# Normalized probabilities computed by GpSimd, block choice one token tile later, three slots of scores: one stage of a two-layer trunk

## The chip, the cores and the metric

The kernel runs on one core of a Trainium2 chip. The time is device microseconds of one execution of the whole program. All times of the profile are microseconds from the start of the span unless marked ns. The engines are TensorE (PE, and PEld for its weight loads), VectorE (DVE), ScalarE (ACT), GpSimd (POOL) and SyncE (SP), which issues the transfers.

## The reference, cut to what matters

The program computes two transformer layers over 1024 tokens of width 1024. The change sits in the second layer's mixer, in the part that attends to compressed keys and chooses blocks of keys for the attention that follows:

```
n_cmp = (S - CMP_LEN) // CMP_STRIDE + 1                      # 63 compressed keys
s_c = einsum('bgjtd,bgnd->bgjtn', q, k_cmp) * scale - slopes * dist_c
s_c = where(dist_c >= 0, s_c, -inf)
e_c = exp(s_c - max(s_c)); l_c = sum(e_c)
p_c = e_c / where(l_c > 0, l_c, 1.0)
o_cmp = einsum('bgjtn,bgnd->bgjtd', p_c, v_cmp)
importance = einsum('bgjtn,nm->bgtm', p_c, overlap)          # 16 blocks of 64 keys
score = where(blk > cur, -inf, where(forced, inf, importance))
top_s, top_i = top_k(score, 8)
```

There are 16 heads in 4 groups (g) of 4 (j), and all arithmetic here is fp32.

## The kernel before, in words

The program is a row of stages, one behind the other. Each ends when all its engines and its last transfer have ended, and the next stage's first transfers are issued only then. The change touches one stage, compress_select_stage. Its first part (projection of the compressed keys and values) is left as it is. Its second part is a loop over 8 token tiles of 128 tokens (i = 0 to 7), with 128 tokens in the partitions and 16 heads x 64 compressed keys = 1024 columns. The engines run it side by side, each through its own instruction list in a fixed order, tied by semaphores. The work of tile i, with the short names that this text uses and the lines of the profile:

- bias(i), GpSimd, L2036 to L2045: the distance penalty and the mask, into one of two slots.
- S(i), TensorE, `scores`, L2094: 8 products of queries and compressed keys into ps_s (two slots of PSUM).
- M(i), VectorE, `maxima`, L2222 and L2225: adds the bias into s (SBUF, two slots), and takes the maximum of each head.
- E(i), ScalarE, `exps`, L2166: 16 exponentials in place in s, one per head, each with its row sum.
- R(i), VectorE, first part of `normalize`, L2230 and L2236 (L2234 for tile 0): reciprocal of the sums, and a copy of it.
- N(i), VectorE, last instruction of `normalize`, L2240: s times the reciprocal, into pn (two slots).
- T(i), TensorE, `transposes`, L2104: 8 transposes of pn into ps_t (one slot).
- K(i), ScalarE, `take`, L2174: ps_t copied to pt in SBUF.
- V(i), TensorE, `values`, L2114: 8 products of pt and the compressed values into ps_o (one slot).
- C(i), VectorE, `pick`, L2250 to L2268, only for i = 4 to 7: group sums of pn, scores of the blocks, the best eight, and a mask in sel.
- O(i), VectorE, `output`, L2275: ps_o times the gates, into the stage's result.

The lists of the loop are, one iteration i:

```
VectorE   R(i) N(i)  C(i) if i >= 4  O(i-1)  M(i+2)      (M(0) M(1) in front; O(7) behind)
TensorE   T(i)  V(i-1)  S(i+2)                           (S(0) S(1) in front; V(7) behind)
ScalarE   E(i)  K(i-1)
GpSimd    bias(i+2)                                      (bias(0) bias(1) in front)
```

At the end TensorE transposes sel (L2130) when all choices are made, ScalarE copies that to blocks (L2183), and SyncE writes blocks to memory (L2011). That transfer is the stage's last work.

Of the kernel before, what the change touches and what calls it, by code (L numbers as in the profile page):

```python
# [20 lines left out]
ALU = mybir.AluOpType  # L21
ACT = mybir.ActivationFunctionType
AX = mybir.AxisListType

P = 128
# [1900 lines left out]
def compress_select_stage(nc, kvT, pe, w1, w2, k_gain, gate_cols, qT, gates, selT, mixed, ident, slopes):  # L1926
# [12 lines left out]
    with Stage(nc, "cmpsel") as st:  # L1939
# [18 lines left out]
        bias = st.sb("bias", [P, 2, C_HEADS, CMP_PAD])  # L1958
        alive = st.sb("alive", [P, 1])
        force = st.sb("force", [P, TT, N_SLC])  # L1960
        s, pn = (st.sb(x, [P, 2, C_HEADS, CMP_PAD]) for x in ("s", "pn"))
        pt = st.sb("pt", [P, 2, PAIRS, P])
        top1, rowsum, rl, rla = (st.sb(x, [P, 2, C_HEADS]) for x in ("top1", "rowsum", "rl", "rla"))
        both = st.sb("both", [P, G, 1 + CMP_PAD])
# [49 lines left out]
        @block.gpsimd  # L2014
        def _(pool):
            nc.gpsimd.memset(t_in[HD:P, :, 0:COLS].rearrange("p v (g t) -> p v g t", t=SEQ)[:, :, :, SEQ - HALF:SEQ], 0.0).then_inc(tail_set, 1)
            pool.wait_ge(tail_set, 1)
            nc.gpsimd.memset(t_in[:, :, COLS + HALF:COLS + 2 * HALF], 0.0).then_inc(tail_set, 1)
            pool.wait_ge(tail_set, 2)
            nc.gpsimd.memset(kcp[:], 0.0).then_inc(zeroed, 1)  # L2020
            nc.gpsimd.memset(vcp[:], 0.0).then_inc(zeroed, 1)
            for h in range(C_HEADS):
                ins = nc.gpsimd.memset(nslope[:, h:h + 1], -slopes[h])
            ins.then_inc(slopes_set, 1)
            nc.gpsimd.memset(alive[:], 1.0).then_inc(alive_set, 1)
            pool.wait_ge(alive_set, 1)
            nc.gpsimd.affine_select(out=alive[:], in_=alive[:], compare_op=ALU.is_ge, fill=0.0, base=-(CMP_LEN - 1),
                                    pattern=[[0, 1]], channel_multiplier=1).then_inc(alive_set, 1)
            nc.gpsimd.memset(both[:], 0.0).then_inc(both_set, 1)
            nc.gpsimd.memset(blocks[:].bitcast(F32), 0.0).then_inc(blocks_set, 1)  # L2030
            pool.wait_ge(slopes_set, 1)

            def make_bias(i):
                if i >= 2:
                    pool.wait_ge(biased, i - 1)
                nc.gpsimd.iota(dist_i[:, i % 2, :], pattern=[[-CMP_STRIDE, CMP_PAD]], base=i * P - (CMP_LEN - 1),  # L2036
                               channel_multiplier=1).then_inc(dist_done, 1)
                pool.wait_ge(dist_done, 2 * i + 1)
                nc.gpsimd.tensor_copy(dist[:, i % 2, :], dist_i[:, i % 2, :]).then_inc(dist_done, 1)
                pool.wait_ge(dist_done, 2 * i + 2)  # L2040
                nc.gpsimd.tensor_tensor(bias[:, i % 2, :, :],
                                        dist[:, i % 2, :].rearrange("p (o n) -> p o n", o=1).to_broadcast([P, C_HEADS, CMP_PAD]),
                                        bcast(nslope[:].rearrange("p (h o) -> p h o", o=1), CMP_PAD), ALU.mult).then_inc(bias_step, 1)
                pool.wait_ge(bias_step, i + 1)
                nc.gpsimd.affine_select(out=bias[:, i % 2, :, :], in_=bias[:, i % 2, :, :], compare_op=ALU.is_ge, fill=NEG,  # L2045
                                        base=i * P - (CMP_LEN - 1), pattern=[[0, C_HEADS], [-CMP_STRIDE, CMP_PAD]],
                                        channel_multiplier=1).then_inc(bias_done, 1)

            make_bias(0)
            make_bias(1)  # L2050
            for i in range(TT):
                if i + 2 < TT:
                    make_bias(i + 2)

        @block.tensor
        def _(te):
# [61 lines left out]
            scores(0)  # L2118
            scores(1)
            for i in range(TT):  # L2120
                transposes(i)
                if i:
                    values(i - 1)
                if i + 2 < TT:
                    scores(i + 2)
            values(TT - 1)
            te.wait_ge(biased, TT)
            te.wait_ge(sel_done, TT - FIRST)
# [5 lines left out]
        @block.scalar  # L2134
        def _(act):
            act.wait_ge(peT_ready, 1)
            nc.scalar.activation(t_in[:, :, COLS:COLS + HALF], ps_t[:, 1, 0:2 * HALF].rearrange("p (v l) -> p v l", v=2), ACT.Copy)\
                .then_inc(peT_done, 1)
            for v in range(2):
                act.wait_ge(hid_ready, v + 1)  # L2140
                nc.scalar.activation(pb[:, v:v + 1], ps_s[:, 0, v * BANK + NW:v * BANK + NW + 1], ACT.Copy).then_inc(pb_done, 1)
                act.wait_ge(pb_done, v + 1)
                of = ps_s[:, 0, v * BANK:v * BANK + NW]
                if v == 0:
                    nc.scalar.activation(hid_k[:], of.rearrange("p (g n) -> p g n", g=G), ACT.Silu, bias=pb[:, 0:1]).then_inc(hid_done, 1)
                else:
                    nc.scalar.activation(hid_v[:, :, 0, :], of.rearrange("p (g n) -> p g n", g=G), ACT.Silu, bias=pb[:, 1:2])
                    nc.scalar.activation(hid_v[:, :, 1, :], of.rearrange("p (g n) -> p g n", g=G), ACT.Silu, bias=pb[:, 1:2])\
                        .then_inc(hid_done, 1)
            act.wait_ge(c_ready, 1)  # L2150
            nc.scalar.activation(sq[:], ps_o[0:CMP_PAD, 0, 0:G * HD].rearrange("p (g d) -> p g d", d=HD), ACT.Square).then_inc(sq_done, 1)
            act.wait_ge(norm, 2)
            nc.scalar.activation(root[:], ms[:], ACT.Sqrt).then_inc(norm, 1)
            act.wait_ge(g_in, 16)
            nc.scalar.activation(gates[:], g_raw[:], ACT.Sigmoid).then_inc(norm, 1)
            act.wait_ge(c_ready, 2)
            act.wait_ge(zeroed, 2)
            for half in range(2):
                rows = slice(half * HD, half * HD + HD)
                nc.scalar.activation(vcp[rows, :, rows], ps_o[rows, 1, 0:G * HD].rearrange("p (g d) -> p g d", d=HD), ACT.Copy)\  # L2160
                    .then_inc(vcp_done, 1)

            def exps(i):
                act.wait_ge(top1_done, i + 1)
                for h in range(C_HEADS):
                    ins = nc.scalar.activation(s[:, i % 2, h, :], s[:, i % 2, h, :], ACT.Exp, bias=top1[:, i % 2, h:h + 1],  # L2166
                                               accum_out=rowsum[:, i % 2, h:h + 1])
                ins.then_inc(e_done, 1)

            def take(i):  # L2170
                act.wait_ge(t_done, i + 1)
                if i >= 2:
                    act.wait_ge(o_done, i - 1)
                nc.scalar.activation(pt[:, i % 2, :, :], ps_t[:].rearrange("p b (m c) -> p (b m) c", c=P), ACT.Copy).then_inc(pt_done, 1)  # L2174

            for i in range(TT + 1):
                if i < TT:
                    exps(i)
                if i:
                    take(i - 1)  # L2180
            act.wait_ge(selT_ready, 1)
            act.wait_ge(blocks_set, 1)
            nc.scalar.activation(blocks[:, FIRST * P:SEQ], ps_s[0:G * N_SLC, 0, 0:SEQ - FIRST * P], ACT.Copy).then_inc(selT_taken, 1)  # L2183

        @block.vector
        def _(dve):
# [30 lines left out]
            def maxima(i):  # L2217
                dve.wait_ge(s_done, i + 1)
                dve.wait_ge(bias_done, i + 1)
                if i >= 2:  # L2220
                    dve.wait_ge(pn_done, i - 1)
                nc.vector.tensor_tensor(s[:, i % 2, :, :], ps_s[:, i % 2, :].rearrange("p (h n) -> p h n", n=CMP_PAD),  # L2222
                                        bias[:, i % 2, :, :], ALU.add).then_inc(biased, 1)
                dve.wait_ge(biased, i + 1)
                nc.vector.tensor_reduce(top1[:, i % 2, :], s[:, i % 2, :, :], AX.X, ALU.max, negate=True).then_inc(top1_done, 1)  # L2225

            def normalize(i):
                at = 2 * i
# [5 lines left out]
                    nc.vector.tensor_scalar(rla[:, 0, :], rl[:, 0, :], alive[:, 0:1], None, ALU.mult).then_inc(link, 1)  # L2234
                else:
                    nc.vector.tensor_copy(rla[:, i % 2, :], rl[:, i % 2, :]).then_inc(link, 1)  # L2236
                dve.wait_ge(link, at + 2)
                if i >= 2:
                    dve.wait_ge(t_done, i - 1)
                nc.vector.tensor_tensor(pn[:, i % 2, :, :], s[:, i % 2, :, :],  # L2240
                                        bcast(rla[:, i % 2, :].rearrange("p (h o) -> p h o", o=1), CMP_PAD), ALU.mult)\
                    .then_inc(pn_done, 1)

            def pick(i):
                at = 7 * (i - FIRST)
# [35 lines left out]
            maxima(1)  # L2281
            for i in range(TT):
                normalize(i)
                if i >= FIRST:
                    pick(i)
                if i:
                    output(i - 1)
                if i + 2 < TT:
                    maxima(i + 2)
            output(TT - 1)  # L2290


# [114 lines left out]
```

## Time and profile before

| | |
|---|---|
| time before, median of 3 runs | 3548.34 us (3542.65 to 3552.97) |
| time of the profiled execution | 3534.34 us |
| its span | 3532.6 us |
| the loop over token tiles in it | 2022.77 to 2116.80 us |
| TensorE, VectorE, ScalarE, GpSimd busy, share of the span | 90%, 44%, 33%, 2% |

A share of busy time is an average over all stages; the loop in question is 94 us of the span. GpSimd's busy time in the whole program is 53.8 us.

### The profile page before, as it was taken

The page shows a single profiled execution, that of the slowest core. Times are in us where ns is not written, and L with a number is a line of the kernel's source. Part 1 is how long each engine was busy: PE and PEld are TensorE (multiplying, and loading weights), DVE is VectorE, ACT ScalarE, POOL GpSimd, SP SyncE. Part 2 cuts the span into 40 slices and gives each one's busy share as a digit, 9 for nine tenths or more (in the row PEclk, how much of TensorE's full clock was granted, in tenths as well). Part 3 has the DMA queues.
Part 4 walks back from the last instruction along what each step waited for, and adds up shares of the span by engine and source line. Part 5 has one row for each costly group of instructions (what it writes and reads, how often), then busy time and mean ns, then how long its engine had stood idle before and what let it go on. Part 6 is the DMA issues. An engine that isn't in the chain of part 4 may idle for free. (4 is left out here: it accounts for less than half of the span.)

```text
span 3532.6 us, 43297 instructions
## 1 busy us (share of the span) xinstructions
PE 3171.4 (90%) x15498; PEld 2612.6 (74%) x15498; DVE 1563.7 (44%) x3383; ACT 1181.6 (33%) x2349; POOL 53.8 (2%) x103
## 2 busy tenths in 40 slices
PE   8998576888899999999999656998998899999999
PEld 6887475666688888887888455776777788888887
DVE  3132766665323232313542066887885323232323
ACT  5232332553221121212442154665664212121211
POOL 0000000000000000000000120000000000000000
PEclk9999787999999999999999677999999999999999
DMA  4333101322122121212363602211201112121212
GB/s 143 106 108 106 37 17 43 65 64 78 48 58 74 48 77 54 84 36 66 91 177 81 123 4 64 65 33 33 64 2 54 42 48 90 42 75 57 78 48 96
DMA packets 266161, 236.79 MB, mean 67 GB/s; under 512 B 44296, under 2 KB 206088, under 8 KB 265960
## 3 DMA queue, kind: packets, MB, share of 16 engines
q1 hardware_dynamic: 265960, 234.18, 23.8%
q8 instruction: 117, 1.92, 0.2%
q14 instruction: 84, 0.69, 0.1%
HBM read 188.80 MB, written 45.15 MB: 66 GB/s over the span
## 5 line engine op out<-in xcount | busy, mean ns | idle before, releaser
L442 PE MATMUL ffn_acc<-m_hi,ffn_w_hi 128*128 128x512 f32 x1408 | 438.4, 392 | 18.6 <-DVE ffn_w_lo L523 18.6
L442 PE MATMUL ffn_acc<-m_lo,ffn_w_hi 128*128 128x512 f32 x1408 | 439.3, 393 | 0.0
L523 DVE TENSOR_TENSOR ffn_w_lo<-ffn_raw,ffn_w_hi 128x1024 fp32r<-128x1024 f32 x88 | 107.9, 1226 | 747.5 <-ACT ffn_w_hi L482 747.5
L442 PE MATMUL ffn_acc<-m_hi,ffn_w_lo 128*128 128x512 f32 x1408 | 437.9, 392 | 0.0
L482 ACT ACTIVATE ffn_w_hi<-ffn_raw 128x1024 fp32r<-128x1024 f32 x88 | 93.3, 1060 | 760.0 <-PE ffn_acc L442 747.1
L1120 PE MATMUL in_acc<-in_w_hi,in_hT_hi 128*128 128x512 f32 (+1 forms) x832 | 331.0, 398 | 0.0
L1122 PE MATMUL in_acc<-in_w_hi,in_hT_lo 128*128 128x512 f32 (+1 forms) x832 | 325.1, 391 | 0.0
L1121 PE MATMUL in_acc<-in_w_lo,in_hT_hi 128*128 128x512 f32 (+1 forms) x832 | 324.7, 390 | 0.0
L442 PEld LDWEIGHTS ffn_acc<-m_hi,ffn_w_hi 128*128 128x128 f32 x1408 | 265.2, 189 | 78.1 <-DVE ffn_w_lo L523 19.4
L442 PEld LDWEIGHTS ffn_acc<-m_hi,ffn_w_lo 128*128 128x128 f32 x1408 | 265.1, 188 | 59.6
L442 PEld LDWEIGHTS ffn_acc<-m_lo,ffn_w_hi 128*128 128x128 f32 x1408 | 265.4, 189 | 58.3
L1765 ACT ACTIVATE at_pr<-at_ps_s 128x512 f32<-128x512 f32 (+3 forms) x384 | 207.8, 541 | 233.0 <-PE at_ps_s L1694 226.5
L462 PE MATMUL ffn_acc_d<-ffn_d_hi,ffn_a_hi 128*128 128x512 f32 x704 | 273.9, 389 | 0.0
L464 PE MATMUL ffn_acc_d<-ffn_d_hi,ffn_a_lo 128*128 128x512 f32 x704 | 273.9, 389 | 0.0
L463 PE MATMUL ffn_acc_d<-ffn_d_lo,ffn_a_hi 128*128 128x512 f32 x704 | 273.9, 389 | 0.0
L1870 DVE TENSOR_TENSOR at_p_lo<-at_pr,at_p_hi 128x512 fp32r<-128x512 f32 (+3 forms) x384 | 232.5, 616 | 68.8 <-ACT at_p_hi L1772 68.4
L1673 PE MATMUL at_ps_m<-at_ka,at_qa 96*128 96x512 f32 (+1 forms) x480 | 181.7, 396 | 63.7 <-DVE at_top L1854 36.9
L1772 ACT ACTIVATE at_p_hi<-at_pr 128x512 fp32r<-128x512 f32 (+3 forms) x384 | 219.1, 572 | 0.0
L493 ACT ACTIVATE ffn_d_hi<-ffn_d_raw 128x512 fp32r<-128x512 f32 x176 | 108.4, 629 | 278.1 <-PE ffn_acc_d L464 278.1
L1694 PE MATMUL at_ps_s<-at_qb,at_kb 128*128 128x512 f32 (+1 forms) x480 | 173.3, 361 | 22.4 <-DMA at_qa<-at_turned 21.0
L528 DVE TENSOR_TENSOR ffn_d_lo<-ffn_d_raw,ffn_d_hi 128x512 fp32r<-128x512 f32 x176 | 117.2, 689 | 160.4 <-ACT ffn_d_hi L493 160.4
L1122 PEld LDWEIGHTS in_acc<-in_w_hi,in_hT_lo 128*128 128x128 f32 x832 | 164.9, 198 | 31.3
(296 smaller groups left out, 5280.1 us busy)
## 6 DMA issues: line engine op xcount, KB each, us to landing
ffn_d_raw<-in_ffn_w_down SPq DMA_DIRECT2D x176, 256.0 KB, 2.8
ffn_raw<-in_ffn_w_gate SPq DMA_DIRECT2D x44, 512.0 KB
ffn_raw<-in_ffn_w_up SPq DMA_DIRECT2D x44, 512.0 KB
in_raw<-in_hy_w_in SPq DMA_DIRECT2D x56, 256.0 KB
proj<-in_nat SPq DMA_DIRECT2D x40, 256.0 KB
in_raw<-in_nsa_w_in SPq DMA_DIRECT2D x40, 256.0 KB
at_qa<-at_turned SPq DMA_DIRECT2D x320, 0.5 KB
at_qa<-q1T_hi SPq DMA_DIRECT2D x16, 264.0 KB
```

What stands on the lines that cost most here:

```text
L442: ins = nc.tensor.matmul(acc[:, m, half, :].rearrange("p (t c) -> p t c", c=P), w[:, m, k, :], h[:, half * S:(half + 1) * S, k, :], start= ...
L462: nc.tensor.matmul(acc_d[:, x, :], a_hi[:, k, rows], d_hi[:, n % R, :], start=k == 0, stop=False)
L463: nc.tensor.matmul(acc_d[:, x, :], a_hi[:, k, rows], d_lo[:, n % R, :], start=False, stop=False)
L464: ins = nc.tensor.matmul(acc_d[:, x, :], a_lo[:, k, rows], d_hi[:, n % R, :], start=False, stop=k == G - 1)
L1120: nc.tensor.matmul(acc[:, n % 4, 0:cols], x_hi, r_hi, start=k == 0, stop=False)
L1121: nc.tensor.matmul(acc[:, n % 4, 0:cols], x_hi, r_lo, start=False, stop=False)
L1122: ins = nc.tensor.matmul(acc[:, n % 4, 0:cols], x_lo, r_hi, start=False, stop=k == KD - 1)
L1673: nc.tensor.matmul(ps_m[:, m % 2, 0:w * P], qa[0:TOP, hh, i * P:(i + 1) * P], ka[0:TOP, s, j * P:(j + w) * P])\
L1694: ins = nc.tensor.matmul(ps_s[:, c % RB, (at + pos) * P:(at + pos + n) * P], lhsT, rhs, start=x == 0, stop=x == len(products) - 1, skip_gr ...
L1765: nc.scalar.activation(pr[:, c % R, 0:w], ps_s[:, c % RB, 0:w], ACT.Exp).then_inc(p_done, 1)
L1772: nc.scalar.activation(p_hi[:, c % R, 0:w], pr[:, c % R, 0:w], ACT.Copy).then_inc(hi_done, 1)
L1870: nc.vector.tensor_tensor(p_lo[:, c % R, 0:w], pr[:, c % R, 0:w], p_hi[:, c % R, 0:w].bitcast(F32), ALU.subtract).then_inc(lo_done, 1)
```

## The change

GpSimd takes over N(i), behind bias(i+2) in its list. VectorE keeps R(i). VectorE's choice C moves one iteration later: C(i-1) stands behind R(i), and C(7) and O(7) stand behind the loop. The score buffer s gets a third slot, so M(i) waits for N(i-3) and no longer for N(i-2). TensorE's list has T(i) at the end of the iteration: V(i-1), S(i+2), T(i). N(i) waits in addition for the first instruction of C(i-2), which reads the same slot of pn.

```diff
--- before.py
+++ after.py
@@ -1958,7 +1958,7 @@
         bias = st.sb("bias", [P, 2, C_HEADS, CMP_PAD])
         alive = st.sb("alive", [P, 1])
         force = st.sb("force", [P, TT, N_SLC])
-        s, pn = (st.sb(x, [P, 2, C_HEADS, CMP_PAD]) for x in ("s", "pn"))
+        s, pn = (st.sb(x, [P, n, C_HEADS, CMP_PAD]) for x, n in (("s", 3), ("pn", 2)))
         pt = st.sb("pt", [P, 2, PAIRS, P])
         top1, rowsum, rl, rla = (st.sb(x, [P, 2, C_HEADS]) for x in ("top1", "rowsum", "rl", "rla"))
         both = st.sb("both", [P, G, 1 + CMP_PAD])
@@ -2048,9 +2048,21 @@
 
             make_bias(0)
             make_bias(1)
+
+            def normalized(i):
+                pool.wait_ge(link, 2 * i + 2)
+                if i >= 2:
+                    pool.wait_ge(t_done, i - 1)
+                if i - 2 >= FIRST:
+                    pool.wait_ge(sel_link, 7 * (i - 2 - FIRST) + 1)
+                nc.gpsimd.tensor_tensor(pn[:, i % 2, :, :], s[:, i % 3, :, :],
+                                        bcast(rla[:, i % 2, :].rearrange("p (h o) -> p h o", o=1), CMP_PAD), ALU.mult)\
+                    .then_inc(pn_done, 1)
+
             for i in range(TT):
                 if i + 2 < TT:
                     make_bias(i + 2)
+                normalized(i)
 
         @block.tensor
         def _(te):
@@ -2118,11 +2130,11 @@
             scores(0)
             scores(1)
             for i in range(TT):
-                transposes(i)
                 if i:
                     values(i - 1)
                 if i + 2 < TT:
                     scores(i + 2)
+                transposes(i)
             values(TT - 1)
             te.wait_ge(biased, TT)
             te.wait_ge(sel_done, TT - FIRST)
@@ -2163,7 +2175,7 @@
             def exps(i):
                 act.wait_ge(top1_done, i + 1)
                 for h in range(C_HEADS):
-                    ins = nc.scalar.activation(s[:, i % 2, h, :], s[:, i % 2, h, :], ACT.Exp, bias=top1[:, i % 2, h:h + 1],
+                    ins = nc.scalar.activation(s[:, i % 3, h, :], s[:, i % 3, h, :], ACT.Exp, bias=top1[:, i % 2, h:h + 1],
                                                accum_out=rowsum[:, i % 2, h:h + 1])
                 ins.then_inc(e_done, 1)
 
@@ -2217,12 +2229,12 @@
             def maxima(i):
                 dve.wait_ge(s_done, i + 1)
                 dve.wait_ge(bias_done, i + 1)
-                if i >= 2:
-                    dve.wait_ge(pn_done, i - 1)
-                nc.vector.tensor_tensor(s[:, i % 2, :, :], ps_s[:, i % 2, :].rearrange("p (h n) -> p h n", n=CMP_PAD),
+                if i >= 3:
+                    dve.wait_ge(pn_done, i - 2)
+                nc.vector.tensor_tensor(s[:, i % 3, :, :], ps_s[:, i % 2, :].rearrange("p (h n) -> p h n", n=CMP_PAD),
                                         bias[:, i % 2, :, :], ALU.add).then_inc(biased, 1)
                 dve.wait_ge(biased, i + 1)
-                nc.vector.tensor_reduce(top1[:, i % 2, :], s[:, i % 2, :, :], AX.X, ALU.max, negate=True).then_inc(top1_done, 1)
+                nc.vector.tensor_reduce(top1[:, i % 2, :], s[:, i % 3, :, :], AX.X, ALU.max, negate=True).then_inc(top1_done, 1)
 
             def normalize(i):
                 at = 2 * i
@@ -2234,12 +2246,6 @@
                     nc.vector.tensor_scalar(rla[:, 0, :], rl[:, 0, :], alive[:, 0:1], None, ALU.mult).then_inc(link, 1)
                 else:
                     nc.vector.tensor_copy(rla[:, i % 2, :], rl[:, i % 2, :]).then_inc(link, 1)
-                dve.wait_ge(link, at + 2)
-                if i >= 2:
-                    dve.wait_ge(t_done, i - 1)
-                nc.vector.tensor_tensor(pn[:, i % 2, :, :], s[:, i % 2, :, :],
-                                        bcast(rla[:, i % 2, :].rearrange("p (h o) -> p h o", o=1), CMP_PAD), ALU.mult)\
-                    .then_inc(pn_done, 1)
 
             def pick(i):
                 at = 7 * (i - FIRST)
@@ -2281,12 +2287,13 @@
             maxima(1)
             for i in range(TT):
                 normalize(i)
-                if i >= FIRST:
-                    pick(i)
+                if i > FIRST:
+                    pick(i - 1)
                 if i:
                     output(i - 1)
                 if i + 2 < TT:
                     maxima(i + 2)
+            pick(TT - 1)
             output(TT - 1)
```

The lists of one iteration are then: VectorE R(i), C(i-1) if i > 4, O(i-1), M(i+2); TensorE V(i-1), S(i+2), T(i); ScalarE as before; GpSimd bias(i+2), N(i).

## Rows read from the trace of the kernel before

**Rows 1.** The page: busy time and share of the span, by engine.
```profile
PE 3171.4 (90%) x15498; PEld 2612.6 (74%) x15498; DVE 1563.7 (44%) x3383; ACT 1181.6 (33%) x2349; POOL 53.8 (2%) x103
```

**Rows 2.** Windows, the loop alone: length, busy by engine, granted clock, DMA share, GB/s.
```profile
2022.77:2116.80 94.03, 51.45 (x308) 49.50 (x306) 62.58 (x116) 51.26 (x265) 24.76 (x24) 0.78 0.00 1
```

**Rows 3.** Waits in the loop: who waited for whom, total us, times, longest.
```profile
PE cmpsel_ps_t L2104 <- DVE cmpsel_pn L2240: 40.3, 8, 8.4
ACT cmpsel_s L2166 <- DVE cmpsel_top L2225: 36.8, 7, 7.0
DVE m_mixed L2275 <- PE cmpsel_ps_o L2114: 18.8, 8, 5.5
```

**Rows 4.** Timeline of VectorE: start, length, operation, idle before and its releaser.
```profile
2030.72 0.25 DVE L2230 RECIPROCAL cmpsel_rl<-cmpsel_rowsum 128x16 f32<-128x16 f32 x1 [3.09 <-ACT cmpsel_s L2166]
...
2037.26 1.23 DVE L2222 TENSOR_TENSOR cmpsel_s<-cmpsel_ps_s,cmpsel_bias 128x1024 f32<-128x1024 f32 x1 [4.41 <-PE cmpsel_ps_s L2094]
...
2039.65 0.24 DVE L2230 RECIPROCAL cmpsel_rl<-cmpsel_rowsum 128x16 f32<-128x16 f32 x1
2039.93 1.13 DVE L2236 COPY cmpsel_rla<-cmpsel_rl 128x16 f32<-128x16 f32 x1
2041.09 1.23 DVE L2240 TENSOR_TENSOR cmpsel_pn<-cmpsel_s,cmpsel_rla 128x1024 f32<-128x1024 f32 x1
...
2048.88 1.23 DVE L2222 TENSOR_TENSOR cmpsel_s<-cmpsel_ps_s,cmpsel_bias 128x1024 f32<-128x1024 f32 x1 [0.56 <-PE cmpsel_ps_s L2094]
...
2078.14 1.97 DVE L2250 TENSOR_REDUCE cmpsel_both<-cmpsel_pn 128x256 f32<-128x1024 f32 x1
...
2082.30 0.20 DVE L2268 TENSOR_SCALAR cmpsel_sel<-cmpsel_marked 128x64 f32<-128x64 f32 x1
...
2106.08 0.17 DVE L2236 COPY cmpsel_rla<-cmpsel_rl 128x16 f32<-128x16 f32 x1
...
2115.56 1.23 DVE L2275 TENSOR_TENSOR m_mixed<-cmpsel_ps_o,gates 128x1024 f32<-128x1024 f32 x1 [2.21 <-PE cmpsel_ps_o L2114]
```

**Rows 5.** Timeline of TensorE in the loop.
```profile
2042.37 1.97 PE L2104 MATMUL cmpsel_ps_t<-ident,cmpsel_pn 128*128 128x128 f32 x8 [5.15 <-DVE cmpsel_pn L2240]
2044.13 2.92 PE L2114 MATMUL cmpsel_ps_o<-cmpsel_vcp,cmpsel_pt 128*128 128x128 f32 x16
2046.89 1.95 PE L2094 MATMUL cmpsel_ps_s<-cmpsel_kcp,cmpsel_q 128*128 128x128 f32 x16
...
2079.81 3.62 PE L2114 MATMUL cmpsel_ps_o<-cmpsel_vcp,cmpsel_pt 128*128 128x128 f32 x16
...
2089.62 1.14 PE L2104 MATMUL cmpsel_ps_t<-ident,cmpsel_pn 128*128 128x128 f32 x8 [4.20 <-DVE cmpsel_pn L2240]
...
2113.50 2.02 PE L2114 MATMUL cmpsel_ps_o<-cmpsel_vcp,cmpsel_pt 128*128 128x128 f32 x16 [1.41 <-DVE m_mixed L2275]
```

**Rows 6.** Timeline of ScalarE: first exponential of tile 4, K(3), the copy to blocks.
```profile
2063.99 0.35 ACT L2166 ACTIVATE cmpsel_s<-cmpsel_s,cmpsel_top 128x64 f32<-128x64 f32 x1 [6.27 <-DVE cmpsel_top L2225]
...
2069.30 1.01 ACT L2174 ACTIVATE cmpsel_pt<-cmpsel_ps_t 128x1024 f32<-128x1024 f32 x1
...
2116.00 0.59 ACT L2183 ACTIVATE cmpsel_blocks<-cmpsel_ps_s 64x512 fp32r<-64x512 f32 x1 [5.40 <-PE cmpsel_ps_s L2130]
```

**Rows 7.** Timeline of GpSimd in the loop.
```profile
2038.56 0.18 POOL L2036 IOTA cmpsel_dist_i<- 128x64 int32 x1 [7.00 <-DVE cmpsel_s L2222]
...
2039.12 1.90 POOL L2041 TENSOR_TENSOR cmpsel_bias<-cmpsel_dist,cmpsel_nslope 128x1024 f32<-128x1024 f32 x1
2041.17 2.15 POOL L2045 TENSOR_SCALAR_AFFINE_SELECT cmpsel_bias<-cmpsel_bias 128x1024 f32<-128x1024 f32 x1
```

**Rows 8.** Windows of 2 us, columns as in rows 2 (the granted clock is third from the end).
```profile
2044.00:2046.00 2.00, 2.00 (x11) 2.00 (x10) 0.00 (x0) 2.00 (x9) 0.00 (x0) 0.50 0.00 0
...
2114.00:2116.00 2.00, 1.96 (x18) 1.69 (x16) 0.44 (x1) 0.00 (x1) 0.00 (x0) 1.00 0.00 0
```

**Rows 9.** Timeline of SyncE: the stage's last transfer.
```profile
2116.61 0.51 SPq L2011 DMA_DIRECT2D selT<-cmpsel_blocks  x1
```

## The prediction

> **What bounds the kernel now.** I read the page first: TensorE is busy for 90% of the span, GpSimd for 2% [rows 1]. Neither figure says anything on this change, since it touches one loop of 94 us, so I went to the windows of that loop. There no engine is near full: of 94.03 us TensorE is busy 51.45, VectorE 62.58, ScalarE 51.26, GpSimd 24.76, and the transfers nothing [rows 2]. A loop in which nobody is busy and no transfer runs is a chain of hand-overs. The waits say which: TensorE waits 40.3 us in 8 waits for N, ScalarE 36.8 us for the maxima, VectorE 18.8 us for V [rows 3].
>
> One turn of the chain can be followed in the timelines. M(2) starts at 2037.26, R(1) at 2039.65 (2.39 later), T(1) at 2042.37 (2.72 later: reciprocal 0.24, copy 1.13, product N 1.23), V(0) at 2044.13 (1.76), S(3) at 2046.89 (2.76), M(3) at 2048.88 (1.99) [rows 4, 5]. The sum is 11.62 us, and each step starts as the one before ends: VectorE and TensorE take turns. The exponentials E(i) are no part of it, as they run beside it. The cause lies in two orders: S(i+2) stands behind T(i) and V(i-1) in TensorE's list, and R(i+1) and N(i+1) stand behind M(i+2) in VectorE's. The loop's 94.03 us are 11.8 for each of the 8 tiles [rows 2].
>
> TensorE's clock is part of the cost. It is at its lower level (0.50, 1.2 GHz) in 2044 to 2046, though TensorE is full there, some 2 us after T(1) ended a wait of 5.15, and at the upper (1.00, 2.4 GHz) in 2114 to 2116 [rows 8, 5]; over the loop it averages 0.78 [rows 2]. V takes 3.62 us in one place and 2.02 in another, T 1.97 and 1.14 [rows 5].
>
> **The change, part by part.**
>
> *The new order on TensorE* takes away the turn-taking. S(i+2) needs only that M(i) has read its slot of PSUM, which is long past, and V(i-1) needs K(i-1). T(i) waits for N(i), but now with S(i+2) done ahead of it, so M(i+2) runs on VectorE beside T(i), K(i) and V(i). What is left on TensorE is the cycle V, S, T, K, since V(i) stands right behind T(i) and must wait for ScalarE's copy: at the upper clock 2.02 + 1.95 + 1.14 + 1.01 [rows 5, 6] and about 0.1 of hand-overs, 6.2 us. Queued behind the waiting T(i) are V(i) and S(i+3), which need it or have time.
>
> *ScalarE* needs for a tile E and K: the first exponential of tile 4 starts at 2063.99, K(3) behind it at 2069.30, so 5.31 + 1.01 = 6.32 us [rows 6]. The cycle K(i-2), V, S, M(i+1), E(i+1), K(i) is 2.02 + 1.95 + 2.43 + 5.31 + 1.01 + 0.2 = 12.9 us for two tiles, 6.5 us a tile. This is the largest of these cycles, so I take 6.5 us for tiles without a choice.
>
> *The product on GpSimd.* The trace has no N on GpSimd. Its nearest row is the bias product, of the same operation, type and size, with two inputs of which both are repeated: 1.90 us against VectorE's 1.23 [rows 7, 4]. I take 1.95. Below, it can't be worth more than 0 where it is hidden; above I take twice the row, 3.8 us, as s is read in full where that row repeats both inputs. GpSimd's load is then bias (from 2038.56 to 2043.32, 4.8 us, of which 1.0 falls away, below) 3.7 + 1.95 = 5.7 us a tile, under 6.5. N(i) is hidden: it ends 2.5 us after R(i) starts, and R(i) starts as K(i-1) ends, while TensorE first does V(i-1) and S(i+2), 4.1 us, so that 1.6 us are left. With 4 us for N, 0.4 us of it shows in each tile, 3 us in all. With 6 us GpSimd needs 9.7 a tile, 3.2 above 6.5 for four tiles: 13 to 14 us in all.
>
> The Trainium skill (GPSIMD Engine Reference, Engine selection) says to leave two-input elementwise work to VectorE, as GpSimd is about twice as slow. Its table's 4497 ns for 2048 elements would make N about 2.2 us, an estimate from that page; the row of the bias product gives 1.90, and the sum is the same by both, as either is hidden.
>
> *The collisions of GpSimd and VectorE.* The 16-element copy takes 1.13 us at 2039.93, and it ends when the bias product (2039.12 to 2041.02) ends; at 2106.08, with GpSimd idle, it takes 0.17 [rows 4, 7]. The mask behind that product starts at 2041.17 beside N on VectorE, and takes 2.15. So each blocked the other for about 1 us. After the change N has left VectorE, so the mask has no such partner. bias(i+3) follows N(i) directly and ends 6.1 us after R(i) starts, just ahead of the copy of R(i+1). If they still meet, the copy costs 1.0, which the 1.6 us in front of T(i) covers. The two small additions in C (inputs in SBUF) start 2.4 us behind its first reduction, when N(i) has just ended.
>
> *VectorE with the choice.* C(i) takes from 2078.14 to 2082.50, 4.36 us [rows 4]. Moved, it runs while N(i) runs on GpSimd, but in VectorE's list it still stands in front of O(i-1) and M(i+2). The load is R 0.5 + C 4.4 + O 1.23 + M 2.43 = 8.5 us, above 6.5, but this holds for one iteration only (i = 5), since the last M is M(7). Iterations 6 and 7 have no M and go by VectorE's R, C and O.
>
> *The third slot* lets M(i) start ahead of N(i-2); without it M(i+2) would wait for N(i), which would cost up to 2 us a tile.
>
> **The sum as a timeline.** M(0), E(0) and R(0) stay (R(0) at 2030.72 [rows 4]). N(0) ends at 2033.3, T(0) at 2035.3; E(1) ends at 2035.9, K(0) at 2037.0. V(0), S(3), T(1) find the clock still low or rising: 3.6 + 2 + 1.3, K(1) ends at 2045. Then three steps of 6.5: K(2) 2051.5, K(3) 2058, K(4) 2064.5. R(5) is at 2064.6 too; the 8.5 us iteration brings R(6) to 2073.1, as M(7) ends. E(7) runs from there to 2078.5, and R(6), C(5), O(5) bring R(7) to 2079.3. Behind R(7) VectorE has R 0.5, C(6) 4.4, O(6) 1.2, C(7) 4.4: 2089.9. Sel's transposes 0.6 and the copy to blocks 0.59 [rows 6]: 2091.1. Before, the last transfer was issued at 2116.61 [rows 9]. The gain is 25.5 us. The last stretch gives a little back: C(6) and C(7) both stand behind R(7).
>
> Against its own execution that is 3534.3 - 25.5 = 3508.8 us. The runs' median is 14.0 us above that execution, so against it 3548.3 - 25.5 = **3523 us**. A difference under 0.3% (10.6 us) can't be told from none here.
>
> **The rivals.**
>
> *TensorE's clock stays low.* If it does not rise, as between T(i) and V(i) TensorE idles some 1.1 us each tile, V is 3.6, S up to 2.9 and T 2.0, and the cycle is 9.6 us a tile. The same timeline then ends at 2103.5: a gain of 13, 3535 us. For it: 0.50 at 2044 to 2046 with TensorE full [rows 8]. Against: the idle stretches that came before such low stretches were of 4 to 5 us [rows 5], now they would be of 1.
>
> *Blocking by shared access.* Each N blocks a VectorE instruction with two SBUF inputs or a copy, and the other way round, for 1 to 2 us on the path in every tile: 8 x 1.5 = 12 us given back, gain 13, 3535 us. For it: the 1.13 and the 2.15 [rows 4, 7]. The Trainium skill (SBUF — State Buffer, Who interferes with whom) has the rule that a VectorE instruction with two SBUF inputs contends with a GpSimd one that reads, and that a copy can lock the pair; the trace agrees with 1.13 against 0.17 us.
>
> *Slower: N on GpSimd costs far more than the bias product.* Then GpSimd is the bound with 3.7 + N a tile. At N = 8.1 us it is as slow as the turn of 11.6 now, and from about 9 us the whole is slower by over 10.6 us: 8 x 1.4 more, 3559 us. Against it speaks the 1.90 of the like row. Nothing in the profile speaks for it but that s is read in full.
>
> *The stage's end isn't what the next one waits for*, so nothing changes: 3548 us. Against: the last transfer is issued 0.02 us after the copy to blocks ends [rows 6, 9], and every next stage starts behind it.
>
> **How the numbers follow.** The forecast (gain 18 to 29) has 0.62, the low clock 0.12, the blocking 0.10 (both gains of 10 to 18), no gain or one too small to measure 0.12, GpSimd as a bound and slower 0.04. The first three are faster by over 0.3%, with a small part lost at the 10.6 line that the other cases give back: faster 0.84, same 0.12, slower 0.04. The range: 3548.3 less 29 is 3519, but the runs themselves span 10.3 us and the profiled one lies 14 lower, so the low end is 3508; the high end takes in the gains of 13 with the runs' scatter, 3541. It holds all but about 2 in 10. All lies on one side but the last case, so the likeliest one's own range, 3508 to 3532, is only a little narrower.
>
> **What would show it.** In the profile after: R starts 6 to 7 us apart for tiles 2 to 5, not 11.6; the loop from 2022.8 ends near 2091; T's waits for N fall from 40.3 us to under 15, most of it at the start; GpSimd's N takes 1.9 to 2.3 us; the copy falls to 0.17 in most tiles; the clock in the loop averages over 0.9. The prediction is wrong if N takes over 4 us, if TensorE still waits 5 us for each N, or if the clock stays at 0.78.

## The result and the profile after

The changed kernel takes 3521.84 us in the median of 6 runs (3514.38 to 3529.11), the kernel before 3549.74 (3542.65 to 3553.35, 6 runs): a ratio of 0.993, with a 95% interval of 0.9912 to 0.9949. The forecast was 3523, faster. In a second set of runs the same kernel gave 0.9948 (0.9928 to 0.9968). Both intervals lie wholly below the 0.3% line that the prediction drew.

A first trap lies in the spans: 3532.6 before [the table of before] and 3521.2 after, which is 11.4 us, while the medians differ by 27.9. The loop starts at 2022.77 in the profile before [rows 2] and at 2032.26 in this one, after stages that the change does not touch. In the 14 profiles of this study that start lies between 2022.77 and 2036.98. So from here on the measure is the loop's own length, from the start of M(0) to the issue of the stage's last transfer: 2116.61 - 2022.77 = 93.8 us before [rows 2, 9], and after:

The profile after, timeline of SyncE (last transfer), and the windows of the loop and of four stretches of 2 us (columns as in rows 2; the granted clock is third from the end):

```profile
2102.27 0.51 SPq L2011 DMA_DIRECT2D selT<-cmpsel_blocks  x1
```

```profile
2032.26:2102.24 69.98, 46.36 (x308) 43.33 (x306) 48.66 (x108) 51.27 (x265) 35.80 (x32) 0.80 0.00 1
...
2056.00:2058.00 2.00, 2.00 (x20) 2.00 (x19) 0.81 (x2) 2.00 (x13) 1.77 (x1) 1.00 0.00 0
2060.00:2062.00 2.00, 0.00 (x0) 0.00 (x0) 1.90 (x4) 2.00 (x9) 1.70 (x2) 1.00 0.00 0
2064.00:2066.00 2.00, 2.00 (x11) 2.00 (x11) 0.52 (x1) 2.00 (x14) 1.85 (x3) 0.50 0.00 0
2070.00:2072.00 2.00, 2.00 (x21) 2.00 (x20) 0.77 (x4) 1.80 (x11) 1.38 (x1) 1.00 0.00 0
```

The loop is 70.0 us, 23.8 less than before. ScalarE's busy time is the same 51.3 us, now in 70 us and not in 94: it is the fullest engine of the loop. The average clock has hardly risen, 0.80 against 0.78 [rows 2], so the gain does not come from the clock.

The waits in the profile after that answer to [rows 3]:

```profile
PE cmpsel_ps_o L2126 <- ACT cmpsel_pt L2186: 13.6, 8, 2.9
DVE m_mixed L2281 <- PE cmpsel_ps_o L2126: 9.8, 4, 3.9
ACT cmpsel_s L2178 <- DVE cmpsel_top L2237: 9.1, 4, 7.3
PE cmpsel_ps_t L2116 <- POOL cmpsel_pn L2058: 7.9, 2, 7.0
```

T waited 40.3 us for N in 8 waits; it now waits 7.9 in 2, of which 7.0 are the start. What TensorE waits for now is ScalarE's copy K. The timeline shows one turn of the new chain, TensorE first, then ScalarE, VectorE and GpSimd:

```profile
2055.25 2.05 PE L2126 MATMUL cmpsel_ps_o<-cmpsel_vcp,cmpsel_pt 128*128 128x128 f32 x16 [1.11 <-ACT cmpsel_pt L2186]
2057.13 1.95 PE L2106 MATMUL cmpsel_ps_s<-cmpsel_kcp,cmpsel_q 128*128 128x128 f32 x16
2058.92 1.04 PE L2116 MATMUL cmpsel_ps_t<-ident,cmpsel_pn 128*128 128x128 f32 x8
2062.19 3.26 PE L2126 MATMUL cmpsel_ps_o<-cmpsel_vcp,cmpsel_pt 128*128 128x128 f32 x16 [2.23 <-ACT cmpsel_pt L2186]
2065.24 2.41 PE L2106 MATMUL cmpsel_ps_s<-cmpsel_kcp,cmpsel_q 128*128 128x128 f32 x16
2067.49 1.04 PE L2116 MATMUL cmpsel_ps_t<-ident,cmpsel_pn 128*128 128x128 f32 x8
```

```profile
2055.81 0.35 ACT L2178 ACTIVATE cmpsel_s<-cmpsel_s,cmpsel_top 128x64 f32<-128x64 f32 x1 [0.62 <-DVE cmpsel_top L2237]
...
2061.14 1.00 ACT L2186 ACTIVATE cmpsel_pt<-cmpsel_ps_t 128x1024 f32<-128x1024 f32 x1
...
2070.20 0.35 ACT L2178 ACTIVATE cmpsel_s<-cmpsel_s,cmpsel_top 128x64 f32<-128x64 f32 x1 [0.62 <-DVE cmpsel_top L2237]
```

```profile
2061.80 0.17 DVE L2248 COPY cmpsel_rla<-cmpsel_rl 128x16 f32<-128x16 f32 x1
...
2067.69 1.22 DVE L2234 TENSOR_TENSOR cmpsel_s<-cmpsel_ps_s,cmpsel_bias 128x1024 f32<-128x1024 f32 x1 [0.98 <-POOL cmpsel_bias L2045]
...
2075.91 0.24 DVE L2242 RECIPROCAL cmpsel_rl<-cmpsel_rowsum 128x16 f32<-128x16 f32 x1
...
2084.40 0.24 DVE L2242 RECIPROCAL cmpsel_rl<-cmpsel_rowsum 128x16 f32<-128x16 f32 x1
...
2090.46 0.24 DVE L2242 RECIPROCAL cmpsel_rl<-cmpsel_rowsum 128x16 f32<-128x16 f32 x1
```

```profile
2062.06 1.90 POOL L2058 TENSOR_TENSOR cmpsel_pn<-cmpsel_s,cmpsel_rla 128x1024 f32<-128x1024 f32 x1 [0.20 <-DVE cmpsel_rla L2248]
...
2066.53 1.15 POOL L2045 TENSOR_SCALAR_AFFINE_SELECT cmpsel_bias<-cmpsel_bias 128x1024 f32<-128x1024 f32 x1
```

The reader is to follow E(3) 2055.81, K(2) 2061.14 (5.33 later), V(2) 2062.19 (1.05), S(5) 2065.24 (3.05), M(5) 2067.69 (2.45), E(5) 2070.20 (2.51): 14.39 us for two tiles, 7.2 a tile. V takes 2.05 in one tile and 3.26 in the next, and the two windows say why: the clock is 1.00 (2.4 GHz) in 2056 to 2058, TensorE then idles for 2.23 us, and in 2064 to 2066 it is full at 0.50 (1.2 GHz). The 2.23 us are made up of two waits: T(2) ended at 2059.96, ScalarE began the copy K(2) only when E(3) was through, at 2061.14, and the copy took 1.00. M(5) is put down to GpSimd's bias, which ended at 2067.68, but S(5) had ended only at 2067.65, so this wait costs 0.03 us.

### The profile page after: what moved, and what is told of

Same layout as the page of the kernel before. It is cut to its first block and busy times, and to the rows that moved or that the text cites. A ratio compares the mean times of both kernels' runs of the same rounds, so it can differ in the third digit from the quotient of the medians.

```text
span 3521.2 us, 43297 instructions
## 1 busy us (share of the span) xinstructions
PE 3176.7 (90%) x15498; PEld 2614.6 (74%) x15498; DVE 1549.7 (44%) x3375; ACT 1181.0 (34%) x2349; POOL 64.8 (2%) x111
```

## The experiments

All loop lengths are read as above, from M(0)'s start to the issue of the last transfer. Each comes from one profile; the changed kernel's own three profiles give the scatter. The starts of R(4) to R(7) (the reciprocals in VectorE's timelines) cut a loop into stretches and show where a difference arises. The first choice, C(4), stands behind R(4) or R(5), so all work with choices lies in the last four columns:

| kernel (us) | M(0) to R(4) | to R(5) | to R(6) | to R(7) | to the last transfer | loop |
|---|---|---|---|---|---|---|
| before | 52.56 | 12.52 | 10.50 | 7.45 | 10.81 | 93.8 |
| TensorE's order alone | 37.63 | 10.90 | 9.84 | 7.42 | 11.94 | 77.7 |
| order and late choice | 35.20 | 6.21 | 9.69 | 7.65 | 13.05 | 71.8 |
| changed, first profile | 37.83 | 5.82 | 8.49 | 6.06 | 11.81 | 70.0 |
| changed, second profile | 37.28 | 5.83 | 8.49 | 6.02 | 11.80 | 69.4 |
| changed, third profile | 35.05 | 6.21 | 8.48 | 6.05 | 11.82 | 67.6 |
| GpSimd's product alone | 52.86 | 11.65 | 12.26 | 8.19 | 12.39 | 97.4 |
| choice in its old place | 37.66 | 11.65 | 10.56 | 8.15 | 13.64 | 81.7 |
| product twice | 36.58 | 7.57 | 11.78 | 7.53 | 13.72 | 77.2 |

**How well it repeats.** The changed kernel, unchanged.

> The changed kernel once more, to see how well the loop's length repeats (from the start of the first L2234 to the issue of the stage's last transfer: 70.0 us in the first profile). Both theories: 69 to 71.5 us; if it moves by more than 2 us, differences of that size between the other runs mean nothing. The clock should again alternate, V near 2 us and above 3 us in turn.

Loop 2102.68 - 2033.26 = 69.4 us; V(0) to V(7) take 3.78, 2.05, 3.68, 2.05, 2.05, 2.05, 3.78, 2.05. In the first profile V(4) too was slow. A third profile, with 8 timed runs:

> The changed kernel timed on the same chip as the improved one, for a direct comparison: 0.993 of the kernel before, loop 68 to 70 us.

Ratio 0.9948 (0.9928 to 0.9968), loop 2097.38 - 2029.77 = 67.6 us, a little below the expected band. The loop of one and the same kernel thus lies between 67.6 and 70.0, and differences of 2 us between whole loops are not read. Which V is slow differs from one execution to the next, and most of this scatter goes with it. R(2) to R(4) took 14.40 and 14.38 us in the two profiles with a slow V(2), and 12.76 in the third, where V(2) took 2.05. A slow V(4) costs nothing: the stretch from R(5) to R(6) is 8.49 with V(4) at 3.60 and at 2.05. From R(4) on the three profiles agree within half a microsecond (32.1 to 32.6 us), so there smaller differences can be read.

**TensorE's order alone**, against the kernel before:

```diff
             for i in range(TT):
-                transposes(i)
                 if i:
                     values(i - 1)
                 if i + 2 < TT:
                     scores(i + 2)
+                transposes(i)
```

> The kernel before with only TensorE's list changed to V(i-1), S(i+2), T(i); the product N stays on VectorE, the choice in its old place, two slots of s. Theory A (the turn-taking of VectorE and TensorE was broken by TensorE's order): nearly the whole gain is here, the loop falls from 93.8 to about 75 us, total about 19 us less than before. Theory B (GpSimd's taking over N is what frees VectorE and brings the gain): the loop stays above 85 us.

3528.58 us against 3546.68, ratio 0.9951 (0.9938 to 0.9964); loop 2102.66 - 2024.93 = 77.7 us. This one moved call gives 16.1 of the 23.8 us, although the clock averaged only 0.76. Theory B, that GpSimd's relief is the cause, falls. The total alone could not divide the gain: the interval of this run overlaps those of the full change (0.993 and 0.9948), and it is the loop that sets the two apart. T's waits for N in its profile, with N still on VectorE:

```profile
PE cmpsel_ps_t L2104 <- DVE cmpsel_pn L2240: 7.9, 2, 6.6
```

**The order and the late choice, product on VectorE.** In addition to the edit above:

```diff
                 normalize(i)
-                if i >= FIRST:
-                    pick(i)
+                if i > FIRST:
+                    pick(i - 1)
...
+            pick(TT - 1)
             output(TT - 1)
```

> As the run before, and in addition the choice one iteration later; N still on VectorE. Its difference from the changed kernel is what GpSimd's product is worth. Theory A: loop about 74 us, so the late choice is worth 1 us and GpSimd's product 4. Theory B: still above 85 us.

Loop 2100.38 - 2028.58 = 71.8 us (one total: 3521.83), 5.9 less than with the order alone. Not all of this is the late choice: R(4), ahead of which the two kernels do the same, already comes 2.4 us earlier (V(2) took 3.44 in the run before and 2.05 here). R(4) in the run before, then here:

```profile
2062.56 0.24 DVE L2230 RECIPROCAL cmpsel_rl<-cmpsel_rowsum 128x16 f32<-128x16 f32 x1
...
2063.78 0.24 DVE L2230 RECIPROCAL cmpsel_rl<-cmpsel_rowsum 128x16 f32<-128x16 f32 x1
```

From R(4) on it is 40.1 against 36.6 us, so the late choice is worth 3.5, where 1 was expected: one choice fewer stands in front of an M (4.7 us less from R(4) to R(5)), and the end gives 1.1 back. In the same way GpSimd's product is worth 4.0 to 4.5 us on top (36.6 against 32.1 to 32.6), as expected. It lies in the three stretches behind R(5), each 1.2 to 1.6 us shorter with N on GpSimd: there VectorE is the fullest engine, and N took 1.23 of its time.

**GpSimd's product alone**, as an edit of the changed kernel (the third slot stays):

```diff
             for i in range(TT):
+                transposes(i)
                 if i:
                     values(i - 1)
                 if i + 2 < TT:
                     scores(i + 2)
-                transposes(i)
...
-                if i > FIRST:
-                    pick(i - 1)
+                if i >= FIRST:
+                    pick(i)
...
-            pick(TT - 1)
```

> The changed kernel with TensorE's old list T(i), V(i-1), S(i+2) and the choice in its old place, so that GpSimd's product and the third slot stand alone. Theory A: the turn-taking stays, N is 0.7 us longer on the chain but the copy no longer waits for GpSimd, so the loop is 92 to 99 us and the total within 0.3% of before. Theory B: the loop is below 80 us.

Ratio 1.0013 (0.9996 to 1.003), loop 2134.33 - 2036.98 = 97.4 us, 3.5 more than before. T waits for every N again, 41.9 us in 8 waits as in [rows 3]:

```profile
PE cmpsel_ps_t L2116 <- POOL cmpsel_pn L2058: 41.9, 8, 8.3
```

The move to GpSimd brings nothing by itself. The total can't tell it from the kernel before, and the 3.5 us are seen in one profile only. Theory A's two terms nearly cancel up to R(4), 52.9 us against 52.6: N is 0.67 us longer, but the copy is no longer held up (0.17 against 1.13). What theory A left out comes behind R(4), where VectorE waits for GpSimd's N in front of each of the four choices:

```profile
DVE cmpsel_both L2256 <- POOL cmpsel_pn L2058: 8.2, 4, 2.1
```

Its own N took 4 x 1.23 = 4.9 us there; 3.3 more is what the profile shows from R(4) on (44.5 against 41.3, 3.2).

**The choice in its old place, all else as changed** (the last two hunks above, without the first):

> The changed kernel with the choice back in its old place, behind R(i) of its own tile, N on GpSimd. VectorE must then wait for GpSimd's N(i), about 2 us, in each of the four tiles with a choice, and nothing else is put there. Theory A: loop 76 to 78 us, so that the late choice is worth 7 to 8 us here. Rival (the choice is off the path either way): 69 to 71.

Loop 2113.08 - 2031.42 = 81.7 us, 12 more than the change, past the expected 76 to 78. VectorE's timeline shows it waiting for GpSimd in front of the choice:

```profile
2069.08 0.24 DVE L2242 RECIPROCAL cmpsel_rl<-cmpsel_rowsum 128x16 f32<-128x16 f32 x1
...
2071.66 1.98 DVE L2256 TENSOR_REDUCE cmpsel_both<-cmpsel_pn 128x256 f32<-128x1024 f32 x1 [2.13 <-POOL cmpsel_pn L2058]
...
2080.73 0.24 DVE L2242 RECIPROCAL cmpsel_rl<-cmpsel_rowsum 128x16 f32<-128x16 f32 x1
...
2091.29 0.24 DVE L2242 RECIPROCAL cmpsel_rl<-cmpsel_rowsum 128x16 f32<-128x16 f32 x1
```

R is 11.65 and 10.56 us apart in tiles 4 to 6, against 5.8 and 8.5 after. The wait of 2.0 to 2.1 us is there in all four tiles, 8.2 in all; one total was 3528.49. From R(4) on it is 44.0 us against 32.1 to 32.6. These 11.4 to 11.9 us are about the 8.2 of waits and the 3.5 that the late choice gave with the product on VectorE. So the late choice is not an extra but what GpSimd's product needs.

**Two slots of scores**, all else as changed:

```diff
-        s, pn = (... for x, n in (("s", 3), ("pn", 2)))
+        s, pn = (... for x, n in (("s", 2), ("pn", 2)))
...
-                if i >= 3:
-                    dve.wait_ge(pn_done, i - 2)
+                if i >= 2:
+                    dve.wait_ge(pn_done, i - 1)
```

> The changed kernel with two slots of s in place of three, M(i) waiting for N(i-2) again. The prediction gave the third slot up to 2 us a tile, so a loop of 80 us or more. The rival, read off the profile after: M(i+2) starts behind S(i+2), 1.0 to 3.7 us after N(i) ended in tiles 2 to 4, so nothing waits: loop 69 to 71.5 us, except for a wait of M(2) on N(0) of some 2 us at the start, which E hides.

Loop 2095.70 - 2027.75 = 67.95 us: inside the changed kernel's own band. The third slot buys nothing that shows.

**The product two and four times over.** Before N, GpSimd makes the same product n times (n = 1 and n = 3):

```diff
+                for r in range(n):
+                    nc.gpsimd.tensor_tensor(pn[:, i % 2, :, :], s[:, i % 3, :, :], bcast(...), ALU.mult).then_inc(extra, 1)
+                    pool.wait_ge(extra, n * i + r + 1)
                 nc.gpsimd.tensor_tensor(pn[:, i % 2, :, :], s[:, i % 3, :, :], bcast(...), ALU.mult)
```

> GpSimd makes N twice into the same place, so it costs 3.9 us a tile. Theory A (N is hidden behind V and S): the loop grows by 1 to 3 us, to 71 to 73. Theory B (the product's price is on the path in every tile): it grows by 8 x 1.95 = 15 us, to 85.

Loop 2107.29 - 2030.11 = 77.2 us: 7 to 10 more, between the two theories. Up to R(4) nothing of it is seen (36.6 us, within the changed kernel's 35.1 to 37.8); from R(4) on it is 8.0 to 8.5 us. Two things show. GpSimd is the bound of the tiles with a bias: its N start at 2061.84, 2069.40, 2076.97, 7.57 apart, which is its load of 3.7 + 3.9; from R(4) to R(5) this costs 1.4 to 1.8 us. And in the tiles with a choice, VectorE's copy and small additions are held up while GpSimd multiplies. VectorE, then GpSimd:

```profile
2074.54 1.20 DVE L2253 COPY cmpsel_rla<-cmpsel_rl 128x16 f32<-128x16 f32 x1
...
2078.11 0.89 DVE L2267 TENSOR_TENSOR cmpsel_imp<-cmpsel_quad,cmpsel_both 128x64 f32<-128x64 f32 x1
2079.03 1.89 DVE L2269 TENSOR_TENSOR cmpsel_score<-cmpsel_imp,cmpsel_force 128x64 f32<-128x64 f32 x1
...
2088.82 1.76 DVE L2267 TENSOR_TENSOR cmpsel_imp<-cmpsel_quad,cmpsel_both 128x64 f32<-128x64 f32 x1
...
2103.49 0.27 DVE L2267 TENSOR_TENSOR cmpsel_imp<-cmpsel_quad,cmpsel_both 128x64 f32<-128x64 f32 x1
2103.80 0.23 DVE L2269 TENSOR_TENSOR cmpsel_score<-cmpsel_imp,cmpsel_force 128x64 f32<-128x64 f32 x1
```

```profile
2076.97 1.90 POOL L2060 TENSOR_TENSOR cmpsel_pn<-cmpsel_s,cmpsel_rla 128x1024 f32<-128x1024 f32 x1
2078.95 1.90 POOL L2063 TENSOR_TENSOR cmpsel_pn<-cmpsel_s,cmpsel_rla 128x1024 f32<-128x1024 f32 x1
```

The first addition ends at 2079.00, just past the end of the first product (2078.87); the second ends at 2080.92, past the end of the second (2080.85). With GpSimd idle they take 0.27 and 0.23. In C(4), C(5) and C(6) the additions lose 2.3, 1.5 and 1.5 us, and the copy of R(5) 1.0: 6.3 of the 8 us, more than GpSimd's pace costs.

> GpSimd makes N four times, 7.8 us a tile, with the bias 11.4 us a tile. Theory A: GpSimd becomes the bound of the tiles with a bias and sits ahead of each T, the loop grows to 92 to 98 us, about that of the kernel before; the prediction's break-even of 8.1 us holds. Theory B: 3 x 15 more, 115 us.

Loop 2133.65 - 2033.22 = 100.4 us, more than the 92 to 98 expected and more than the 93.8 of the kernel before. Theory B's 115 is far off. GpSimd's N now come 11.52 us apart, its load of bias and product as expected (3.7 + 7.8). One total was 3556.78, against 3554.63 for one run of before.

**TensorE kept busy in the gap.** Behind T(i), i = 1 to 4, four products that are overwritten later:

```diff
                 transposes(i)
+                if 1 <= i < TT - 3:
+                    te.wait_ge(biased, i + 2)
+                    for m in range(4):
+                        nc.tensor.matmul(ps_s[:, (i + 1) % 2, m * P:(m + 1) * P], q[:, m, i * P:(i + 1) * P], kcp[:, m // 2, :], ...)
```

> Four products of queries and keys are added behind T(i) for i = 1 to 4, into the slot of ps_s that S(i+3) overwrites anyway, so TensorE does not idle while ScalarE copies ps_t. Theory C (the alternating V of 2.05 and 3.3 to 3.8 us comes from TensorE's clock falling in its idle stretches): V(2) and V(4) fall to about 2.05 and the loop is 2 to 3 us shorter, 67 to 68.5, although work was added. Rival D (the slow V come from something else, such as ScalarE reading PSUM at the same time): V stays above 3 in every second tile and the loop is the same or up to 1 us longer.

V(1) to V(5) take 2.05 each; the gap ahead of V(2), 2.23 us in the profile after, is now 1.33:

```profile
2051.42 1.06 PE L2122 MATMUL cmpsel_ps_s<-cmpsel_kcp,cmpsel_q 128*128 128x128 f32 x8
2053.81 2.05 PE L2132 MATMUL cmpsel_ps_o<-cmpsel_vcp,cmpsel_pt 128*128 128x128 f32 x16 [1.33 <-ACT cmpsel_pt L2194]
```

R(2) to R(4) is 2047.32 to 2060.08, 12.76 us, against 14.40 (2055.69 to 2070.09) in the profile after. Theory C holds, rival D falls. The loop of 2092.66 - 2024.80 = 67.9 us is not shorter than the best of the changed kernel, 67.6, which also had a fast V(2): the filling makes regular what otherwise differs from one execution to the next. One run with two gaps filled would not show that by itself, so all profiles with this loop are counted, V(1) to V(4) in each. In the changed kernel (three profiles) and its two-slot twin, 5 of the 8 V behind an idle stretch of 1.8 to 2.2 us were slow, and none of the 8 behind 1.1 to 1.5 us. Here, and in the two runs that follow, the stretch is 1.5 us or less, and none of 12 was slow.

**Scores first.** Two more swaps on the changed kernel:

```diff
-                if i:
-                    values(i - 1)
                 if i + 2 < TT:
                     scores(i + 2)
+                if i:
+                    values(i - 1)
                 transposes(i)
...
-                if i:
-                    output(i - 1)
                 if i + 2 < TT:
                     maxima(i + 2)
+                if i:
+                    output(i - 1)
```

> The changed kernel with two more swaps: TensorE's list S(i+2), V(i-1), T(i), so that S fills the wait for K, and VectorE's M(i+2) ahead of O(i-1). Theory C (the loop goes by the chain K, V, S, M, E, K, and S can leave its place behind V): that chain loses V, ScalarE's own 6.3 us a tile is the next bound, and the loop is 64 to 66 us, against 68 to 70. Rival (the chain only shifts: O(i-1) late holds V(i), and the choices hold VectorE anyway): loop 68 to 70, no gain. In the total this is 4 to 6 us below the changed kernel, too little to be certain by itself.

Loop 2095.99 - 2031.33 = 64.7 us, as expected and clear of the 67.6 to 70.0. In the tiles without a choice ScalarE's copies come 6.2 us apart, about its own load (6.32 in the prediction), and the clock averages 0.89:

```profile
2031.33:2095.99 64.66, 39.79 (x308) 37.59 (x306) 48.76 (x108) 50.84 (x265) 35.80 (x32) 0.89 0.00 1
```

```profile
2050.81 1.01 ACT L2186 ACTIVATE cmpsel_pt<-cmpsel_ps_t 128x1024 f32<-128x1024 f32 x1
...
2057.02 1.02 ACT L2186 ACTIVATE cmpsel_pt<-cmpsel_ps_t 128x1024 f32<-128x1024 f32 x1
```

The total, 3520.01 us (3511.88 to 3527.89) against 3544.27, is 0.9928 (0.9905 to 0.9952). That is the lowest ratio of the study but can't be told from the changed kernel's 0.9948 by these intervals. With TensorE's swap alone:

> Only the swap on TensorE, S(i+2), V(i-1), T(i); VectorE's list as in the changed kernel. Theory C: most of the gain comes once M(i+2) also stands ahead of O(i-1), since O(i-1) waits for V(i-1) in either case; loop 66 to 67.5 us. Rival: 64 to 66, as with both swaps, if M's place does not matter.

Loop 2098.93 - 2033.95 = 65.0 us: M's place does not matter, the rival was right there. With and without it the gain lies ahead of R(4), which comes after 32.0 and 32.4 us against 35.1 to 37.8; from R(4) on both take 32.6, as the changed kernel does.

## Why the prediction was right

*The chain.* Right. The prediction's case is that VectorE and TensorE take turns because of S's place behind T and V; moving T alone gave 16.1 of 23.8 us, and the product alone gave none.

*The number.* The forecast's gain was 25.5 us, and the loop's was 23.8, 24.4 and 26.2 in three profiles. That 3521.84 lies 1.2 us from the 3523 of the forecast is more than the runs can bear out: the ratio's interval stands for a gain of 18 to 31 us, the medians differ by 27.9, and 4 us of that are not in the loop. This nearness is partly luck.

*The timeline.* In the first profile after, counted from M(0), R(7) was forecast at 2079.3 - 2022.8 = 56.5 us and came at 2090.46 - 2032.26 = 58.2; the tail behind it was forecast at 11.8 and took 2102.27 - 2090.46 = 11.8. The iteration with M(7) and a choice was forecast at 8.5 us and took 8.49. The 1.7 us that were missed lie in front.

*The term that was mis-sized: 6.5 us a tile.* The prediction took V at 2.02 and S at 1.95, the upper clock. The chain it named is the one that binds, but V(2) and S(5) met the lower level: 14.39 us for two tiles in place of 12.9, of which V is 1.0 and S 0.5 us. Where V(2) met the upper clock, in the third profile, two tiles took 12.76, so the cycle itself was summed rightly. V(0) and S(3) at the low clock cost 1 us more than the 3.6 + 2 allowed for. So the rival of the low clock was partly true. Its cause is that the idle stretch in front of V is 2.2 us in every second tile, as the copy waits for ScalarE's exponentials, and not the 1.1 that the prediction counted everywhere. The filled gap, and S in its place, take it away. The part of the gain in question is only 1 to 3 us. Two of the prediction's own signs failed on this: the clock averaged 0.80 (0.84 in the other two profiles) and not over 0.9, which in the first profile is hardly above the 0.78 named as a sign of being wrong; and R did not come 6 to 7 us apart but 5.8 and 8.6 in turn, 6.7 on average. The gain came all the same, since it hangs on the order and not on the clock.

*The product on GpSimd.* 1.90 us, as the bias product, and hidden: T waits for N in tiles 0 and 6 only. The slack is not 1.6 us in each tile, though. The prediction had R(i) start as K(i-1) ends; in truth R(3) starts 0.6 us before K(2) ends, and R(4) stands behind M(5), which waits for S(5). So 3.5 us are left between the end of N(3) and T(3), and 0.8 between N(4) and T(4). What the prediction made of a dearer product was too mild: with 4 us it put 3 us, and 7 to 10 were measured with 3.9, because the choice's additions and the copy are then blocked (6.3 us) and GpSimd's whole load (7.57 us a tile) sets the pace. The slower rival's own sum has a slip too: by its load of 3.7 + N against 11.8 a tile, 8 x 1.4 us more needs an N of 9.5 us, not 9. And the low clock's end at 2103.5 comes to about 2102 by the terms given. Neither bears on the forecast. With four products the loop is 6.6 us longer than before, so the break-even lies under 7.8 us, and not at 8.1 (a straight line between the two measured loops puts it at about 6.7, an estimate).

*The collisions.* The copy was forecast to fall to 0.17: it took that in six of the seven tiles and 0.67 in tile 1, the mask 1.15. The blocking itself is shown by the doubled product; in the changed kernel the choice's additions take 0.28 and 0.23, and only tile 1's copy meets it. The Trainium skill's rule (SBUF — State Buffer, Who interferes with whom), that a VectorE instruction with two SBUF inputs contends with a GpSimd one that reads, agrees with the 0.89 and 1.89 us against 0.27 and 0.23.

*The late choice* was costed rightly where it stands (8.5 us in one iteration only, a little given back at the end), but what it saves was given no number. With the product on GpSimd it saves 11.4 to 11.9 us, as otherwise VectorE waits 2 us for N in each of four tiles; with the product on VectorE it gave 3.5.

*The third slot.* Wrong: up to 2 us a tile without it, said the prediction; two slots ran in 67.95 us. From tile 1 on, N(i) starts right behind R(i) and is over before S(i+2) is there; only M(2) waited for N(0), about 2 us at the start, which E(1) hid.

*The end of the stage* does pass on to the total: 23.8 to 26.2 us in the loop, 25 in the first ratio (0.7% of 3549.74) and 18 in the second (0.52% of 3544.27). From the issue of the stage's last transfer to the end of the span it is 1416.0 us before and 1418.9 after.

## What to carry to other kernels

When no engine of a loop is near full and two of them wait for each other in turn, look first for an early, independent step that stands behind a late one in an in-order list. Here one moved call gave two thirds of the gain, and handing work to an idle engine gave nothing until the lists were reordered. Work given to a slower engine also needs its reader moved later: the price of the new hand-over is the wait in front of whoever reads the result in the same iteration. And where the rest of the program scatters by 14 us, measure the stage between two of its own events, and cut it into stretches before putting a difference down to an edit: 2.4 of the 5.9 us between two of these kernels lay ahead of the place where they differ.

## What the runs showed of the hardware

A VectorE addition of 64 elements with both inputs in SBUF, 0.23 us alone, took 1.89 while GpSimd ran a product, and ended 0.07 us after it. GpSimd's product took 1.90 all the same. A VectorE addition with one input in PSUM was not held up: in the profile after, M(6)'s took 1.22 beside a product on GpSimd.

```profile
2073.51 1.22 DVE L2234 TENSOR_TENSOR cmpsel_s<-cmpsel_ps_s,cmpsel_bias 128x1024 f32<-128x1024 f32 x1 [0.56 <-PE cmpsel_ps_s L2106]
```

```profile
2073.04 1.90 POOL L2041 TENSOR_TENSOR cmpsel_bias<-cmpsel_dist,cmpsel_nslope 128x1024 f32<-128x1024 f32 x1
```

TensorE's granted clock fell to 0.50 after idle stretches of 1.8 to 2.2 us in some tiles and not in others of the same kernel (V(2) behind 2.22 us idle took 2.05 in one profile, 3.26 behind 2.23 in another). What decides between the two is not shown. With gaps of at most 1.5 us in the repeating part, V(1) to V(4) were at 2.05 in all three kernels that had them.
